# Down products of the experts: 64-column tiles with 512 moving columns for two slot groups, 32-column tiles for the third

## The reference

```
logits = hf @ w_router;  topv, topi = top_k(logits, 2);  wts = softmax(topv)
gate = sum(one_hot(topi, 8) * wts)
for e in range(8):
    out = out + gate[:, e] * (silu(hf @ wg[e]) * (hf @ wu[e])) @ wd[e]
```

## Time and profile before

| | us |
|---|---|
| median of 3 runs | 1545.43 (1545.17 to 1545.57) |
| profiled execution | 1545.37 |
| its span | 1543.3 |
| PE busy | 1513.5 |
| DVE busy | 522.9 |
| ACT busy | 396.5 |

### The profile page before, as it was taken

How to read it: one execution, slowest core, us unless ns; L and a number is a source line. 1 busy time by engine, 2 the same in 40 slices (tenths; PEclk the granted TensorE clock), 3 DMA queues, 4 the chain that set the end, 5 groups by cost and what they waited for, 6 DMA issues and landing times. The chain is left out here.

```text
span 1543.3 us, 32349 instructions
## 1 busy us (share of the span) xinstructions
PE 1513.5 (98%) x15015; PEld 1006.7 (65%) x15015; DVE 522.9 (34%) x601; ACT 396.5 (26%) x482; POOL 32.4 (2%) x118
## 2 busy tenths in 40 slices
PE   8999999999999999999999999999999999999996
PEld 8999898988888999986344343443443434435433
DVE  5564656565665656542021110110211101101112
ACT  6444455554445344442000000000000000000001
POOL 1000000000000000103000000000000000000000
PEclk9999999999999999999999999999999999999998
DMA  9655653547566555667999999999999999999993
GB/s 351 195 173 180 217 183 98 163 160 229 169 204 203 168 186 176 238 254 321 393 370 396 426 424 426 425 425 426 425 425 426 425 426 425 425 425 425 425 426 154
DMA packets 104492, 478.76 MB, mean 310 GB/s; under 512 B 6212, under 2 KB 31908, under 8 KB 79780
## 3 DMA queue, kind: packets, MB, share of 16 engines
q1 hardware_dynamic: 104356, 476.68, 78.8%
HBM read 475.61 MB, written 1.05 MB: 309 GB/s over the span
## 5 line engine op out<-in xcount | busy, mean ns | idle before, releaser
L1715 PE MATMUL ps<-unit,h_slots 128*32 128x448 f32 x5376 | 511.2, 539 | 0.0
L1715 PEld LDWEIGHTS ps<-unit,h_slots 128*32 128x32 f32 x5376 | 172.4, 110 | 322.2 <-issue 319.0
L930 DVE TENSOR_TENSOR wlo<-raw,whi 128x2048 fp32r<-128x2048 f32 (+1 forms) x116 | 259.0, 2236 | 169.3 <-ACT whi L590 169.1
L1737 PE MATMUL ps<-unit,act_tok 128*32 128x256 f32 x4704 | 259.3, 379 | 11.9 <-DVE act_tok L1292 8.9
L590 ACT ACTIVATE whi<-raw 128x2048 fp32r<-128x2048 f32 (+1 forms) x116 | 216.7, 1869 | 132.1 <-PE ps L1374 78.0
L1374 PE MATMUL ps<-a_parts,whi 128*128 128x256 f32 x1280 | 231.2, 283 | 0.0
L1737 PEld LDWEIGHTS ps<-unit,act_tok 128*32 128x32 f32 x4704 | 151.1, 110 | 120.7 <-DVE act_tok L1292 12.3
L1374 PEld LDWEIGHTS ps<-a_parts,whi 128*128 128x128 f32 x1280 | 199.8, 192 | 0.2
L1374 PE MATMUL ps<-a_parts,wlo 128*128 128x256 f32 x640 | 181.1, 283 | 0.0
L1288 DVE TENSOR_TENSOR act_tok<-act_tok,ps 128x896 f32<-128x896 f32 x18 | 19.2, 1067 | 352.3 <-PE ps L1715 352.3
L1374 PEld LDWEIGHTS ps<-a_parts,wlo 128*128 128x128 f32 x640 | 122.8, 192 | 0.0
(11 more groups left out here) (252 smaller groups left out, 1326.6 us busy)
## 6 DMA issues: line engine op xcount, KB each, us to landing
unit<-in_w_e_gate SPq DMA_DIRECT2D x64, 1792.0 KB, 28.6
unit<-in_w_e_up SPq DMA_DIRECT2D x64, 1792.0 KB, 27.2
unit<-in_w_e_down SPq DMA_DIRECT2D x64, 1792.0 KB, 29.2
raw<-in_w_in SPq DMA_DIRECT2D x32, 1024.0 KB, 5.7
raw<-in_w_ff_gate SPq DMA_DIRECT2D x10, 1024.0 KB, 5.3
raw<-in_w_ff_up SPq DMA_DIRECT2D x10, 1024.0 KB, 5.4
raw<-in_w_xk SPq DMA_DIRECT2D x8, 1024.0 KB, 5.2
raw<-in_w_xv SPq DMA_DIRECT2D x8, 1024.0 KB, 5.1
```

The source lines that it names most:

```text
L930: dve.tensor_tensor(wlo[n % SPL][:, 0:size], raw[n % RAW][:, 0:size], whi[n % SPL][:, 0:size].bitcast(F32), ALU.subtract).then_inc(s["lo_r ...
L1715: ins = pe.matmul(ps[q * QP:(q + 1) * QP, 2 * h + f, 0:HC], he[:, k, c0 + h * QP:c0 + (h + 1) * QP], w[:, q * QC + f * HC:q * QC + (f + 1) ...
L1737: ins = pe.matmul(o[q * QP:(q + 1) * QP, h * 256:(h + 1) * 256], act_t[:, h, j * QP:(j + 1) * QP], unit_t[i - part + u][:, c0:c0 + 256], s ...
```

## The change

`act_tok` holds the blocks of groups 0 and 1 side by side for each j (`act_two`, 64 columns per j), and those of group 2 behind them. Silu, products and transposes write and read through `act_of[h]`. In `down`, groups 0 and 1 become one 128x64 stationary block; two matmuls of 512 moving columns write the halves of the output columns to partitions 0..63 and 64..127 of bank 6. The third group keeps four 128x32 matmuls of 256 columns, into bank 7. In the first down unit the first products wait for the transposes of both groups; all j of the two groups come ahead of those of the third. The copies to `y_slots` become one of 64x512 and, with three groups, two of 32x256 on each of ACT and DVE.

```diff
-    act_t = moe("act_tok", [P, SG, QC], F32, work)
+    act_t = moe("act_tok", [P, SG * QC], F32, work)
+    act_two = act_t[:, 0:2 * QC].rearrange("p (j g c) -> p j g c", g=2, c=QP)
+    act_of = [act_two[:, :, g, :] for g in range(2)]
+    act_of.append(act_t[:, 2 * QC:].rearrange("p (j c) -> p j c", c=QP))
...
+        def y_pieces(half, n_groups):
+
+            both = (y32[0:HP, half * C:(half + 1) * C], bank(6)[half * HP:(half + 1) * HP, :])
+            if n_groups == SG - 1:
+                return [both]
+            third_group = slice(HP, HP + QP)
+            return [both] + [(y32[third_group, q * 256:(q + 1) * 256], bank(7)[q * QP:(q + 1) * QP, 0:256])
+                             for q in (2 * half, 2 * half + 1)]
...
-                    for q in range(2):
-                        for g in range(n_groups):
-                            ins = copy(y_rows(g, q), y_piece(g, q))
+                    for dst, src in y_pieces(0, n_groups):
+                        ins = copy(dst, src)
...
-                        dst = act_t[:, h, :].rearrange("p (j f c) -> p j f c", f=2, c=QP // 2)
+                        dst = act_of[h].rearrange("p j (f c) -> p j f c", f=2)
...
-                        for c0, n in (((0, HC), (HC, HC)) if in_two else ((0, QC),)):
-                            blocks = act_t[:, h, c0:c0 + n]
+                        for j0, j1 in (((0, R // 2), (R // 2, R)) if in_two else ((0, R),)):
+                            blocks = act_of[h][:, j0:j1, :]
                             dve.transpose(blocks, blocks).then_inc(s["actT_ready"], 1)
...
-                    def row_products(h, j):
+                    def two_groups(j):
+
+                        for half in range(2):
+                            ins = pe.matmul(bank(6)[half * HP:(half + 1) * HP, :], act_t[:, j * HP:(j + 1) * HP],
+                                            piece(j, half * C, C), start=j == 0, stop=j == R - 1, skip_group_check=True)
+                        return ins
+
+                    def third_group(j):
 
                         for q in range(4):
-                            u, c0 = divmod(j * D + q * 256, DFE)
-                            ins = pe.matmul(o[q * QP:(q + 1) * QP, h * 256:(h + 1) * 256], act_t[:, h, j * QP:(j + 1) * QP],
-                                            unit_t[i - part + u][:, c0:c0 + 256],
-                                            start=j == 0 and h % 2 == 0, stop=j == R - 1, skip_group_check=True)
+                            ins = pe.matmul(bank(7)[q * QP:(q + 1) * QP, 0:256], act_of[2][:, j, :],
+                                            piece(j, q * 256, 256), start=j == 0, stop=j == R - 1, skip_group_check=True)
                         return ins
...
-                        for h in range(n_groups):
-                            ins = row_products(h, j0 + middle)
-                        ins.then_inc(s["unit_used"], 1)
+                        if n_groups == SG:
+                            third_group(j0 + middle)
+                        two_groups(j0 + middle).then_inc(s["unit_used"], 1)
...
-                    for h in range(n_groups):
+                    if part == 0:
+                        pe.wait_ge(s["actT_ready"], third(v, 1, n_groups))
+                    for j in whole:
+                        ins = two_groups(j)
+                    if n_groups == SG:
                         if part == 0:
-                            pe.wait_ge(s["actT_ready"], third(v, h, n_groups))
+                            pe.wait_ge(s["actT_ready"], third(v, 2, n_groups))
                         for j in whole:
-                            ins = row_products(h, j)
+                            ins = third_group(j)
```

More of the change, by code:

```diff
@@ L1246, in y_lo @@
                     dve.wait_ge(s["unit_used"], every(v, BODY, U0))
-                    for q in range(2, 4):
-                        for g in range(n_groups):
-                            ins = dve.tensor_copy(y_rows(g, q), y_piece(g, q))
+                    for dst, src in y_pieces(1, n_groups):
+                        ins = dve.tensor_copy(dst, src)
                     ins.then_inc(s["ydve_done"], 1)
@@ L1730, in down, with piece @@
                     unit_landed(i, v)
-                    o = ps[:, 6:8, :].rearrange("p a b -> p (a b)")
-                    def row_products(h, j):
+                    def piece(j, c0, n):
+                        u, w0 = divmod(j * D + c0, DFE)
+                        return unit_t[i - part + u][:, w0:w0 + n]
+                    def two_groups(j):
[4 more added lines that the diff above has]
+                    def third_group(j):
                         for q in range(4):
-                            u, c0 = divmod(j * D + q * 256, DFE)
-                            ins = pe.matmul(o[q * QP:(q + 1) * QP, h * 256:(h + 1) * 256], act_t[:, h, j * QP:(j + 1) * QP],
-                                            unit_t[i - part + u][:, c0:c0 + 256],
-                                            start=j == 0 and h % 2 == 0, stop=j == R - 1, skip_group_check=True)
+                            ins = pe.matmul(bank(7)[q * QP:(q + 1) * QP, 0:256], act_of[2][:, j, :],
+                                            piece(j, q * 256, 256), start=j == 0, stop=j == R - 1, skip_group_check=True)
                         return ins
@@ L1812, in _ @@
                 used = groups_of(NE - 1) * QP
-                for q in range(2):
-                    for g in range(groups_of(NE - 1)):
-                        ins = act.activation(y_rows(g, q), y_piece(g, q), ACT.Copy)
+                for dst, src in y_pieces(0, groups_of(NE - 1)):
+                    ins = act.activation(dst, src, ACT.Copy)
                 ins.then_inc(s["tail_y32"], 1)
@@ L1832, in _ @@
                 used = groups_of(NE - 1) * QP
-                for q in range(2, 4):
-                    for g in range(groups_of(NE - 1)):
-                        ins = dve.tensor_copy(y_rows(g, q), y_piece(g, q))
+                for dst, src in y_pieces(1, groups_of(NE - 1)):
+                    ins = dve.tensor_copy(dst, src)
                 ins.then_inc(s["tail_y32d"], 1)
```

## The result

| | before | changed |
|---|---|---|
| median of 4 runs each, us | 1545.47 | 1561.04 (1560.23 to 1562.04) |
| profiled execution, us | 1545.37 | 1561.63 |
| its span, us | 1543.3 | 1559.7 |

The ratio is 1.0103, 95% interval 1.0090 to 1.0116: the kernel got 15.6 us slower. The forecast was slower by 7.1 us, 1552.5, with a range to 1558.5.

A forecast was written before the change was run, and what follows sets the result against it. TensorE was taken as the bound: 2.3 + 3.8 - 1.2 + 7.5 = +12.4 us, less 3.5 absorbed by weight waits, less 0.9 and 0.95 at the end, made +7.05 us: 1552.5 us, range 1544.5 to 1558.5.

The forecast's parts named there:

- the halves side by side: In the down products, both 512-column halves overlap: 0.430 us a set, 0.860 instead of 0.866 us per j, -1.2 us.
- the waits for weights that vanish: In the last visit, three waits for down weights absorb 3.5 us of TensorE's added time.
- DVE's transposes: Transposes of act_tok keep their element counts and only get a stride of 64; costed at nothing, 1.11 us each.
- the tail: After the last down product: -0.9 us from shorter copies and -0.95 us if the clock stays up in the scatter.
- I take 0.10 us for each change.: In the down products, each exposed change between 64 and 32 columns costs 0.10 us, 7.5 us together.
- The count of 75: Exposed changes of tile width: 72 in three-group visits and 3 on leaving the light visits.
- The waits were priced as time standing still alone: First down products wait for group 1: +0.46 us in five visits, +1.28 us in three light ones; 2.3 and 3.8 us.
- free changes: Rival: changes of tile width in the down products cost nothing, giving 1544.9 us; chance 0.18.
- the halves in turn: Rival: the 64-column halves don't run side by side, 0.86 us more per j, +193 us, about 1746 us; chance 0.05.
- Changes of 0.2 us: Rival: each change of tile width in the down products costs 0.2 us, giving 1560.0 us; chance 0.07.
- The end by DMA: Rival: DMA sets the end and, with fewer instruction packets, finishes 2.6 us sooner; kernel takes 1540.9 us; chance 0.04.

The follow-up runs named there:

- e5: Kernel before, with 64-column tiles and the single 64x512 copies in the last visit and its tail alone; 1543.80 against 1545.16 us, ratio 0.9988.
- e9: Kernel before, first down products also waiting for group 1's transposes, 12 identity matmuls filling that wait in the three light visits; 1548.29 against 1545.01 us.
- e2: Changed kernel with 12 unused identity matmuls ahead of the transposes' wait in the three light visits; 1557.86 us, ratio 1.0080 to the kernel before.
- e7: Changed kernel with odd down units reordered for fewer width changes and 12 identity matmuls in the light visits' wait; 1553.25 against 1545.16 us before.
- e10: Kernel before, with 64-column tiles and 64x512 copies in the three two-group visits alone; 1550.35 against 1545.01 us, ratio 1.0033.
- e3: Changed kernel with two-group and third-group products alternating at every j from down part 1 on, 140 more width changes; 1582.22 us, ratio 1.0237.
- e1: Changed kernel with odd down units reordered, the third group's four j first, for fewer width changes; 1557.81 against 1544.87 us before, ratio 1.0086.
- e4: Kernel before with one edit: the first down products wait for group 1's transposes too; 1552.88 us, ratio 1.0046.

## Why the prediction was wrong

Right were the bound and the direction. TensorE set the pace, and the lateness of its last down product is the sum of the visits' losses: it ends 18.1 us later, 1545.6 instead of 1527.5 us. Right, too, were the halves side by side (0.430 us a pair), the waits for weights that vanish (the 3.5 us, confirmed by e5 and e9), DVE's transposes (1.11 us as before), and the tail, 14.1 instead of 15.8 us from that product to the span's end, -1.7 against -1.85: ACT's copy took 0.59 us and the clock was at 1.00 through nearly all of the scatter.

```profile
1546.05 0.59 ACT L1829 ACTIVATE y_slots<-ps 64x512 f32<-64x512 f32 x1 [52.52 <-PEq L358]
```

```profile
1549.00:1550.00 1.00, 1.00 (x5) 1.00 0.00 0
1550.00:1551.00 1.00, 0.54 (x3) 0.77 0.00 0
```

That the clock stayed up there was in part luck. The same tail with the same pause has the fall in the scatter or just ahead of it in e2, e5, e7 and e10, and takes 14.6 to 14.8 us there. A window of e2's scatter:

```profile
1544.00:1545.00 1.00, 1.00 (x3) 0.50 0.00 0
```

Two steps failed. They stand here with the lateness of TensorE's last product, forecast at 12.4 - 3.5 = 8.9 us:

- **"I take 0.10 us for each change."** The term was mis-sized: a change costs 0.14 us (0.28 for two in the trace of the change, 0.287 in e3's, 0.144 by e3's time, 0.14 by e1's). The gap is as forecast, 0.10 to 0.11. What I left out is behind it: the weight loads of the new width start with its first matmuls and not ahead of them, and the second set follows the first 0.02 us late on 32 columns and 0.05 us late on 64. The earlier trace rows had it, in the 0.34 us between the first two scatter matmuls where the later ones are 0.235 apart; I used that row for a rival and not for the value. The count of 75 holds in the trace; at 0.044 us more each, that is 3.3 us. The eight waits add 0.09 us each, 0.7 us: after the longer standstill TensorE starts 0.15 us behind the end of the transpose (791.66 against 790.40 + 1.11), where it starts 0.05 us behind it in the earlier trace rows and in the filled waits of e2. Why was not found. Together 4.0 us.
- **The waits were priced as time standing still alone.** In a light visit all idle time before the first product now lies in one piece. The pause of 3.6 us in the tail of the earlier trace rows had brought the clock down, the light visits' new pause is 3.3 us, and I used that row only for the tail, where it gave a gain. A fall costs 1.4 to 1.7 us. e2 and e9 take the falls in the waits away, and the time goes with them. The profiled execution has three falls in the expert stage, 4.8 us, and 3.2 of them are in such waits.

4.0 + 4.8 = 8.8 of the 18.1 - 8.9 = 9.2 us. Another 0.2 us is there before the first expert product (716.98 against 716.78), and some 0.1 us between the down products of one visit and those of the next, besides the changes of width there. The third of the falls, in visit 6, comes without a pause, in a gather that the change does not touch; it is in the profiled executions of the change, e3, e4 and e9 and in none of the others. Why it comes there was not found, so 1.6 us of the loss stay without a cause.

The rivals: free changes and the halves in turn are out. Changes of 0.2 us (1560.0 us) came nearest in time, but for the wrong reason, as e3 has them at 0.14. The end by DMA could not come to pass, though the instruction packets fell from 118 to 97, as that rival had counted.

## What to carry to other kernels

Price a change of tile width by the time from steady stream to steady stream, not by the gap alone, and count the changes before choosing an order: larger tiles save next to nothing here (0.860 against 0.866 us per j), and every change costs 0.14 us. When an edit merges several short waits of TensorE into one, look for the clock behind it, and if the pause can't be avoided, fill it with matmuls whose results nobody reads. Where TensorE waits for weights in one place only, at the end, a slower order is free there and nowhere else: the same edit gave 1.4 us in the last visit and took 15.6 over all visits.

## What the hardware showed that was not expected

- Granted clock at 0.50 in visit 6 at the end of 32 gather matmuls of 96 moving columns, which start 0.11 us apart and leave no idle time, in four of the twelve traces; in the kernel before the same gather runs at 1.00 throughout.
- A standstill of 3.2 us in the light visits of the changed kernel brought the clock down in visits 1 and 7 and not in visit 4 of one execution; in e1 it came down in all three.
- In visit 1 of e10 the clock stayed at half for 6 us and more, through products without a pause, where elsewhere in these traces it came back after some 3.4 us.
